# Packed ring for the experts' weights, gate columns computed inside the delta rule's last head, and more PSUM banks for transposed probabilities

## The reference, cut to what matters

```python
# first block: softmax attention of 8 query heads, 768 keys, over latent and context tokens
p = jax.nn.softmax(s, axis=-1); o = einsum('bhgqk,bhkd->bhgqd', p, v)
...
# second block, one projection for several uses; z is 1024 columns, the gates 2048
qkv, z, alpha, beta, c_q, c_kv, k_rope, gates = jnp.split(h @ w_in, IN_OFFSETS, axis=-1)
o_dn = delta rule over chunks, 8 heads, two directions (a scan: S_t needs S_{t-1})
y    = rms_norm(o_dn, norm_g) * jax.nn.silu(z)
...
# latent attention, 8 heads, 512 queries, 768 keys; k and q are rms-normed, tails rotated (rope)
k = rms_norm(concat([k_nope, k_pe]), k_norm_g); p = softmax(q @ k.T * scale); o = p @ v
...
# experts: 16 experts, each takes the 64 tokens with the highest affinity to it
affinity = jax.nn.softmax(h @ router_w, axis=-1); gate, idx = lax.top_k(affinity.T, 64)
hid = jax.nn.silu(xe @ w_gate) * (xe @ w_up)        # w_gate, w_up: 1024 x 1408 per expert
out = zeros.at[idx].add((hid @ w_down) * gate)      # w_down: 1408 x 1024 per expert
```

## Time and profile before

| what | value |
|---|---|
| median of 3 runs | 4580.68 us (4578.31 to 4581.77) |
| profiled execution, its own time | 4588.09 us |
| span of its instructions | 4586.3 us, mean granted clock 0.940 |
| `even_attention` | 317 to 552 us |
| `delta_mixer` | 2335 to 3035 us |
| `linear` in2 | 3041 to 3209 us |
| `mla`: to `sums(43)`, `spread`, units | 3214 to 3379, to 3432, to 3614 us |
| `route` | 3819 to 3873 us |
| `experts` | 3873 to 4586 us |

### The profile page before, as it was taken

The page is one execution under the profiler, slowest core; times in us unless marked ns, Lnnn a source line. Parts: engine busy times, 40 slices in busy tenths (PEclk is TensorE's granted clock), DMA queues, the critical chain, the costliest instruction groups (busy, mean ns, idle before and its releaser), DMA issues. The chain is left out here.

```text
span 4586.3 us, 46385 instructions
## 1 busy us (share of the span) xinstructions
PE 4115.6 (90%) x18567; PEld 2460.8 (54%) x18567; DVE 1674.2 (37%) x2954; ACT 874.8 (19%) x1650; POOL 742.6 (16%) x505
## 2 busy tenths in 40 slices
PE   6997789999979998899989999879988896998988
PEld 3664445554446765687457777744544445433433
DVE  2245443225724453433746666610123313010111
ACT  3123320000123333200123333310113201000000
POOL 0003212223401110222414333300002200000000
PEclk8998999999989999999989999979979897999999
DMA  4115511114421111542520010022100312999999
GB/s 161 37 66 208 181 37 55 59 52 148 168 69 37 42 38 47 184 166 99 181 59 24 21 29 8 6 87 101 53 0 1 147 42 96 382 395 396 407 403 365
DMA packets 315325, 579.68 MB, mean 126 GB/s; under 512 B 55676, under 2 KB 181340, under 8 KB 314472
## 3 DMA queue, kind: packets, MB, share of 16 engines
q1 hardware_dynamic: 315112, 576.70, 34.2%
HBM read 566.02 MB, written 10.63 MB: 126 GB/s over the span
## 5 line engine op out<-in xcount | busy, mean ns | idle before, releaser
L2879 PE MATMUL dn_ps<-room,dn_w 128*128 128x512 f32 (+1 forms) x640 | 231.6, 516 | 4.8 <-DVE dn_qx L3350 2.5
L737 PE MATMUL ffn_up_ps<-room,ffn_up_w 128*128 128x384 f32 (+1 forms) x704 | 210.0, 442 | 11.9 <-DMA ffn_up_w<-in_ffn_w_gate 11.9
L737 PE MATMUL ffn_up_ps<-ffn_up_t,room 128*128 128x384 f32 (+1 forms) x704 | 205.7, 436 | 0.8 <-DVE room L817 0.8
L737 PE MATMUL ffn_up_ps<-room 128*128 128x384 f32 (+1 forms) x704 | 203.9, 433 | 0.0
L4358 PE MATMUL experts_ps<-experts_ring,experts_xs 128*64 128x512 f32 (+1 forms) x768 | 165.4, 583 | 29.2 <-DMA experts_ring<-in_w_up 29.2
L4358 PE MATMUL experts_ps<-experts_ring,room 128*64 128x512 f32 (+1 forms) x768 | 162.8, 578 | 13.9 <-DMA experts_ring<-in_w_up 13.3
L160 PE MATMUL in_ps<-in_w,room 128*128 128x512 f32 x384 | 167.9, 600 | 8.1 <-DMA in_w<-in_w_in 8.0
L2342 PE MATMUL hgrn_ps<-room,hgrn_w 128*128 128x512 f32 x384 | 174.4, 594 | 0.0
L737 PEld LDWEIGHTS ffn_up_ps<-room,ffn_up_w 128*128 128x128 f32 x704 | 135.6, 194 | 71.4 <-DMA ffn_up_w<-in_ffn_w_gate 12.7
L4393 PE MATMUL experts_ps<-experts_ring,experts_hidT 128*64 128x512 f32 x704 | 161.1, 615 | 12.0 <-DMA experts_ring<-in_w_down 6.8
L2879 PEld LDWEIGHTS dn_ps<-room,dn_w 128*128 128x128 f32 x640 | 120.3, 193 | 95.9 <-issue 83.2
(11 more groups left out here) (605 smaller groups left out, 7176.3 us busy)
## 6 DMA issues: line engine op xcount, KB each, us to landing
experts_ring<-in_w_gate SPq DMA_DIRECT2D x128, 704.0 KB, 11.2
experts_ring<-in_w_up SPq DMA_DIRECT2D x128, 704.0 KB, 12.5
experts_ring<-in_w_down SPq DMA_DIRECT2D x160, 512.0 KB, 7.7
ffn_down_w<-in_ffn_w_down SPq DMA_DIRECT2D x55, 1024.0 KB, 4.7
att_wm<-in_mod_w SPq DMA_DIRECT2D x20, 2048.0 KB, 9.0
ffn_up_wm<-in_ada_w SPq DMA_DIRECT2D x12, 2048.0 KB, 12.3
ffn_up_w<-in_ffn_w_up SPq DMA_DIRECT2D x22, 1024.0 KB, 7.7
ffn_up_w<-in_ffn_w_gate SPq DMA_DIRECT2D x20, 1024.0 KB, 5.2
```

Source lines behind the costliest of these rows:

```text
L737: mm = nc.tensor.matmul(result(n, p), lhs[:, k, :], rhs[:, k, :], start=k == 0, stop=k == half - 1)
L2879: mm = nc.tensor.matmul(out, wt[:, h % 2, piece, k, :], hT[:, k, tok], start=k == 0, stop=k == KD - 1)
```

## The change

**Attention of the first block.** Job 1 of `turn` uses bank 7, jobs 0 and 2 bank 6; all copies are ACT's, behind `exponents(u + 1)`. Job 1 waits until bank 7 is free (`other_free`), job 2 for the copy of job 0. Whoever uses bank 7 next waits for the copy of job 1.

**Delta rule.** 768 of the 1024 columns of z, for 4 tiles, are computed inside `delta_mixer`: 8 units of 8 matmuls with 384 columns, 8 matmuls in period 8 before `tr_of`, then 3 (once 2) behind each of the chain's operations in period 9, and 3 in period 10. ACT applies silu; SP loads two weight blocks of 1.5 MB in periods 6 and 7 and stores the 8 results in period 9. `linear` has 256 + 2048 columns left.

**Latent attention.** The 8 `kn` scalings and three of the four ropes go beside `lift` and `sums` of u = 37 to 43. The 4 `kp` scalings and the last rope stay behind `sums(43)`. The three jobs of `turn` have banks 4, 5 and 7. The scores of head a wait for that head's exponential alone.

**Route and experts.** `gated` and its transposes move out of `route` into `experts` (`gate_slots` on DVE, eight `turn` fillers in pair 0, where all fillers now stand before the last up step). The ring has 25344 float32 per partition in place of 19712, and pieces are laid end to end, each waiting only for the last piece that it overlaps: 9 up pieces, or 12 down pieces, fit. An up step goes cut by cut, so that silu of cut 0 can start before the others are done; the transposes use banks 0 to 2, the first down matmul waits for the first copy only, and the next pair no longer waits for the result before its first filler.

```diff
+        def turn_bank(m):
+            return OTHER if m == 1 else TURN
...
+            def other_free(u):
+                j, at = divmod(u, TILES)
+                if at == 0 and j:
+                    pe.wait_ge(S["stored"], 2 * j)
+                mods_before = OPENING + LOOP * j + sum(x < at for x in mod_at(j))
+                pe.wait_ge(S["mod_out"], mods_before)
+                if at == 3 and j + 1 < PAIRS:
+                    pe.wait_ge(S["roped"], j + 3)
...
-                if n:
-                    on = jobs[n - 1][2]
-                    pe.wait_ge(S[f"{on}_taken"], (dve_jobs if on == "dve" else act_jobs)[n - 1])
+                if m == 0 and u:
+                    pe.wait_ge(S["taken"], jobs_through[u - 1])
+                if m == 1:
+                    other_free(u)
+                if m == 2:
+                    pe.wait_ge(S["taken"], n - 1)
                 for i in range(4):
                     b, kt = divmod(4 * m + i, n_keys)
-                    mm = nc.tensor.transpose(ps[:, TURN, i * P:(i + 1) * P], probs[:, u % 2, 1 - b, kt * P:(kt + 1) * P], ident)
+                    mm = nc.tensor.transpose(ps[:, turn_bank(m), i * P:(i + 1) * P], probs[:, u % 2, 1 - b, kt * P:(kt + 1) * P], ident)
...
+                if t >= CTX_TILES:
+                    pe.wait_ge(S["taken"], jobs_of[u][1] + 1)
...
+FILL, FILL_BLOCKS = 3 * P, 2
...
+    fill_units = [(n, t) for n in range(FILL_BLOCKS) for t in range(CTX_TILES, TILES)]
+    spots = [(H, 0, "tr")] + [(H + 1, n, at) for n in range(L) for at in (("ks", "tr", "su") if n else ("tr", "ks", "su"))] + [(H + 2, 0, "tr")]
+    fill_at, given = {}, 0
+    for spot in spots:
+        count = KD if spot == spots[0] else 2 if spot == spots[-2] else 3
+        fill_at[spot] = range(given, given + count)
+        given += count
...
+                if H - 2 <= p < H:
+                    n = p - (H - 2)
+                    sp.wait_ge(S["side"], side_n["q", p])
+                    sp.dma_start(wz[:, n, :, :], flat[:, :, QKV + S_Z + n * FILL:QKV + S_Z + (n + 1) * FILL]).then_inc(S["z_in"][n], 16)
+                if p == H + 1:
+                    for u, (n, t) in enumerate(fill_units):
+                        sp.wait_ge(S["z_taken"], u + 1)
+                        sp.dma_start(proj_v[:, t, S_Z + n * FILL:S_Z + (n + 1) * FILL], z_stage[:, u % 4, :]).then_inc(S["z_stored"][u % 4], 16)
...
+            def fill(p, n, at):
+                for step in fill_at.get((p, n, at), ()):
+                    u, k = divmod(step, KD)
+                    piece, t = fill_units[u]
+                    if k == 0:
+                        pe.wait_ge(S["z_in"][piece], 16)
+                        if u == 0:
+                            pe.wait_ge(S["z_start"], H)
+                        elif u < 3:
+                            pe.wait_ge(S["ssq_out"], H)
+                            pe.wait_ge(S["qk_out"], H)
+                        if u >= 2:
+                            pe.wait_ge(S["z_taken"], u - 1)
+                    mm = nc.tensor.matmul(ps[:, u % 2, 0:FILL], hT[:, k, t * P:(t + 1) * P], wz[:, piece, k, :], start=k == 0, stop=k == KD - 1)
+                    if k == KD - 1:
+                        mm.then_inc(S["z_mm"], 1)
...
                 if n == 0:
+                    fill(p, n, "tr")
                     tr_of(n, hc)
                     y_of(n, hi)
                     side("ktr", hi)
                 ks_of(n, hc)
+                fill(p, n, "ks")
                 d_of(n, hi)
                 if n:
                     tr_of(n, hc)
+                    fill(p, n, "tr")
...
+            def z_out(p, n, at):
+                for step in fill_at.get((p, n, at), ()):
+                    u, k = divmod(step, KD)
+                    if k < KD - 1:
+                        continue
+                    act.wait_ge(S["z_mm"], u + 1)
...
+                    nc.scalar.activation(z_stage[:, u % 4, :], ps[:, u % 2, 0:FILL], ACT.Silu).then_inc(S["z_taken"], 1)
...
-        linear(nc, "in2", hT, KD, columns(w_rest, latent, end=S_ALPHA) + columns(w_rest, latent, first=S_GATE), proj,
+        linear(nc, "in2", hT, KD, columns(w_rest, latent, first=S_Z + FILL * FILL_BLOCKS, end=S_ALPHA) + columns(w_rest, latent, first=S_GATE), proj,
...
+    TURNS = (4, 5, 7)
...
+        beside = {37: [("rope", 0)], 38: [("kn", 0)], 39: [("kn", 1), ("kn", 2)], 40: [("rope", 1), ("kn", 3)], 41: [("kn", 4), ("kn", 5)], 42: [("rope", 2), ("kn", 6)], 43: [("kn", 7)]}
...
+            def spread(what, n):
+                if what == "rope":
+                    pe.wait_ge(S["evac"], evac_through[at_unit["qp", n]])
+                    pe.wait_ge(S["q_roped"], n + 1)
+                    nc.tensor.matmul(ps[:, 7, :], swap, qp[:, n, :], start=True, stop=True).then_inc(S["swapped"], 1)
+                    return
+                job = n if what == "kn" else H + n
+                if job == 0:
+                    pe.wait_ge(S["rt_copied"], 4)
+                pe.wait_ge(S["k_scaled"], 2 * job)
+                for half in range(2):
+                    tok = slice(half * N // 2, (half + 1) * N // 2)
+                    if what == "kn":
+                        mm = nc.tensor.matmul(ps[:, 4 + half, 0:N // 2], ident[0:H, n:n + 1].broadcast_to([H, P]), RT[0:H, tok], start=True, stop=True)
...
+                mm.then_inc(S["spread"], 1)
...
+                for job in beside.get(u, ()):
+                    spread(*job)
...
-            pe.wait_ge(S["rt_copied"], 4)
             for i in range(PAIRS):
-                spread(i)
-                pe.wait_ge(S["evac"], evac_through[at_unit["qp", i]])
...
-                nc.tensor.matmul(ps[:, 6 + i % 2, :], swap, qp[:, i, :], start=True, stop=True).then_inc(S["swapped"], 1)
+                spread("kp", i)
+            spread("rope", PAIRS - 1)
 
             def qk(u):
                 i, t = unit_list[u]
-                if u:
-                    pe.wait_ge(S["exp_done"], 2 * u)
+                if t == CTX_TILES:
+                    pe.wait_ge(S["q_roped"], 2 + i)
+                    pe.wait_ge(S["k_scaled"], 2 * (H + i + 1))
                 tok = slice((t - CTX_TILES) * P, (t - CTX_TILES + 1) * P)
                 for a in (1, 0):
+                    if u:
+                        pe.wait_ge(S["exp_done"], 2 * u - a)
...
-                    if n >= 2:
-                        pe.wait_ge(*taken_by(n - 2))
+                    if u:
+                        pe.wait_ge(*taken_by(n - JOBS))
+                    if m == 2 and i:
+                        pe.wait_ge(S["stored"], 2 * (i - 1) + 1)
                     for q in range(4):
                         b, kt = divmod(4 * m + q, TILES)
-                        mm = nc.tensor.transpose(ps[:, 4 + n % 2, q * P:(q + 1) * P], probs[:, u % 2, 1 - b, kt * P:(kt + 1) * P], ident)
+                        mm = nc.tensor.transpose(ps[:, TURNS[m], q * P:(q + 1) * P], probs[:, u % 2, 1 - b, kt * P:(kt + 1) * P], ident)
...
-                own.then(nc.vector.tensor_tensor(by_slot, slot_iota[:, 0:SLOTS].unsqueeze(1).broadcast_to([P, E, SLOTS]),
-                                                 slot[:, m, :].unsqueeze(2).broadcast_to([P, E, SLOTS]), ALU.is_equal))
-                if m >= 2:
-                    dve.wait_ge(S["pick_turned"], 2 * (m - 1))
-                nc.vector.tensor_tensor(gated[:, m % 2, :].rearrange("p (e s) -> p e s", e=E), by_slot,
-                                        aff[:, m, :].unsqueeze(2).broadcast_to([P, E, SLOTS]), ALU.mult).then_inc(S["gated_done"], 1)
-                take(dve, nc.vector.tensor_copy, 2 * m, S["pick_even"])
+                nc.vector.tensor_tensor(by_slot, slot_iota[:, 0:SLOTS].unsqueeze(1).broadcast_to([P, E, SLOTS]),
+                                        slot[:, m, :].unsqueeze(2).broadcast_to([P, E, SLOTS]), ALU.is_equal)
...
-        back = [("scatter", pair - 1, i) for i in range(2 * tiles)] if pair else []
+        back = [("scatter", pair - 1, i) for i in range(2 * tiles)] if pair else [("turn", 0, n) for n in range(2 * tiles)]
...
+            def turn_gates(n, bank):
+                m, part = divmod(n, 2)
+                pe.wait_ge(S["gated_done"], m + 1)
+                for i in range(4):
+                    mm = nc.tensor.transpose(ps[:, bank, i * P:(i + 1) * P], gated[:, m % 2, (4 * part + i) * P:(4 * part + i + 1) * P], ident)
+                mm.then_inc(S["pick_turned"], 1)
...
+                    if not done and pair:
+                        pe.wait_ge(S["out_done"], pair)
...
-                    pe.wait_ge(S["hid_done"], pair)
-                    pe.wait_ge(S["out_done"], pair)
+                    pe.wait_ge(S["hid_done"], len(cuts) * pair)
...
                     for m in range(2 * len(cuts)):
                         for side in range(2):
 
-                            n, c = divmod((m + 3 * side) % 6, 3)
+                            c, n = m // 2, (m % 2) ^ side
                             a, b = cuts[c]
...
```

(35 more changed lines are left out.)

241 lines of the change are left out of this document (106 added, 135 removed).

## The result

The changed kernel takes 4444.94 us (median of 4 runs, 4443.31 to 4448.18) against 4581.23 us before (4 runs); the ratio is 0.9702, with a 95% interval of 0.9685 to 0.9719. The profiled execution took 4443.31 us, its span is 4441.5 us, so 144.8 us less than the span of before; 7 us of this difference is that the profiled execution of before was 7 us above its median.

A forecast was written before the change was run, and what follows sets the result against it. Only the experts were taken as near the transfer rate, elsewhere PE work, low-clock chains or waits; -12 - 33 - 20 - 14 - 39 = -118 us gave a 4463 us median, range 4430 to 4512.

The forecast's parts named there:

- z inside the delta rule: Moving z work from linear into the delta rule: linear -42, delta rule +6 rounded up to +9, net -33 us.
- fills at 1.2 GHz: Delta rule's last head: many short fills with waits don't raise the low clock, +48 us, 4511 us; chance 0.07.
- Route: Gating loop of 18.0 us leaves route, 5.0 us remain there, so the experts start 13 us sooner.
- Ring: Experts' weight transfers: fuller queue, 415 GB/s, last landing 4529 in place of 4568, -39 us including the 13 us earlier start.
- the case that I had kept as a bound: Experts' weight transfers run at 422 GB/s throughout, giving -50 us in place of -39.
- The rival that the wait only moves to TensorE: Experts: the bigger ring only moves the wait to PE, the phase keeps its 397 GB/s, 4485 us; chance 0.09.
- the one on the same bank: Experts' up steps: two sides meeting in one bank serialise, 4.9 us steps take up to 9.8, up to 4710 us; chance 0.03.
- First attention: First block's attention: two banks and copies on ACT remove most of 17.9 us of waits, -12 us.
- ScalarE as a bound: First block's attention: job 0's copy waits behind two exponentials, +24 us and the 12 us gain lost, 4499 us; chance 0.05.
- Turns: Latent attention's units: three banks remove 24.4 us of copy waits, 0.8 us per unit remains in 12 units, -14 us.
- Spread: Latent attention before the first scores: scalings and ropes moved beside projections, 53 us become 34 or 28, -20 us taken.
- price "14 us": Latent attention, u = 37 to 43: 8 kn at 1.4 us and 3 ropes at 0.9 us add 14 us.

The follow-up runs named there:

- the last kernel above: Changed kernel with spread handing over by halves and the experts' first gathers done two ahead of the up step needing them: 4441.76 us, ratio 0.9680.

## Why the prediction was right, point by point

*z inside the delta rule.* Forecast -33, measured -33. The mechanism was right, the exact hit is partly luck, for terms inside moved. A step took 2.38 us, not 2.7: from the start of an operation to its fill it is 0.45 us, not 0.61, and from there to the next operation 1.93, not 2.1, which makes 5 us less over 16 steps. The 2 us that I gave to the covered hole in period 8 did not come: in the trace after, twelve records behind a wait of 2.67 us took 2.57 us, where twelve of the same line take 1.60 elsewhere; before, none was slow behind that wait. And I had rounded +6 up to +9; measured are +8. The rival "fills at 1.2 GHz" is out: 0.95.

*Route.* 13.5 us against 13.

*Ring.* Forecast -26 for the phase behind route, measured -36. The end was right: the transfer never stops. It ran at 421 to 422 throughout, the case that I had kept as a bound, where I had taken 415; that is the 10 us between forecast and result. The reason that I gave did not hold: "the ring holds 13 MB", so that TensorE's pause "no longer empties the queue". The pause itself was nearly gone, and the ring with the slots of before keeps its queue too (418 GB/s); which edit did it, the transposes' banks or the order of the up steps, stays open. I had the shorter pauses only in TensorE's sum (625 us against 636; TensorE was busy 624), not as a reason why the transfer would keep running. The rival that the wait only moves to TensorE is out, and so is the one on the same bank: an up step takes 4.88 us between fillers, as before, and the two groups of 768 records have means of 585 and 572 ns, where they had 583 and 578.

*First attention.* Forecast -12, measured -18 with -11 of idle time. Idle time was sized well, the clock was left out. ScalarE as a bound is out. That the two halves of the part overlap, each taking most of the idle time alone, I had not seen.

*Turns.* Forecast -14, measured -25, of it 12.5 of idle time (the wait for the exponential that I had left at 0.8 us a unit measured 1.1). Here too the term left out is the clock; I had named it in brackets and given it nothing. And I named the banks first; by themselves they win 3.6.

*Spread.* Forecast -20, measured -11. The step that failed is the price "14 us" for 8 `kn` and 3 ropes beside u = 37 to 43: it left the `kn` and the projections beside them at their full speed. In the trace after, three of the projections behind a `kn` take 4.5 us and not 2.8 (the others 2.84). Two of the three:

```profile
3303.35 1.55 PE L3646 MATMUL mla_ps<-cst 8*128 8x384 f32 x4
3304.83 4.54 PE L3609 MATMUL mla_ps<-mla_cqT,mla_big 128*128 128x512 f32 x6
...
3312.87 2.92 PE L3646 MATMUL mla_ps<-cst 8*128 8x384 f32 x4 [1.23 <-DVE mla_kn L3943]
3315.72 4.43 PE L3609 MATMUL mla_ps<-mla_cqT,mla_big 128*128 128x512 f32 x6
```

Three of them cost 5 us, the second `kn` of each couple 1.4 more. The low clock was carried from the chain into the work beside it. It is not the waits: the last kernel above has none there, and its projections behind a `kn` were as slow or slower. What is left is the 8 rows of the `kn`, by exclusion: no kernel was run with more rows in their place.

The sum was near in part by luck, because errors of both signs stood in it: -13 us of clock in the latent attention's units and some -7 in the first attention, -10 in the experts, and +9 where slow work was moved among fast work.

## What to carry to other kernels

In a stage of short matmuls with a wait in each unit, price a removed wait at its idle time and then ask what the clock gives back: here it was as much again in one stage and repeated in eleven profiles. Before a wait is removed from one resource, look what is ready next: three banks without the wait by head won 3.6 of 26 us. And the fill that covers a chain's hand-over pays most: the first one shortened the step by 0.5 us, while the further ones cost 0.48 us each, little less than the 0.63 that they would have cost elsewhere.

## What the runs showed that I had not expected

- The same 1,900 records of the first attention took 161.7 to 173.2 us in ten profiled executions, at a clock of 0.81 to 0.88, while the latent attention's units varied by 1.6 us. A difference of under 10 us in the former is not to be read from one pair of traces.
- Matmuls with 8 rows, 32 records without a gap, were at a clock of 0.51, and projections of full size behind others of this kind took 4.4 to 5.2 us in place of 2.8. Matmuls of 128 rows with a short fill between them were at 1.00. In these rows being busy was not enough. The Trainium skill ("TensorE: Matmul & The Clock Gate", Part 1) has the clock follow how busy the engine has lately been; the row of that stretch, 10.40 us busy of 10.40 at 0.51, does not agree with busy time as the only measure.
- A fill of 0.81 us made a chain's step shorter, 1.93 to 1.42 us, since the operation that follows ran in 0.71 us and not 1.22.
